# RG-LRU stage in another order of units, one subtraction per tile moved to GpSimd, and attention's first units begun block by block

## The chip, the cores and the metric

One NeuronCore of one Trainium2 chip. The metric is device time of one launch in microseconds (us), the median of three runs. Engines: TensorE (PE, its weight loads PEld), VectorE (DVE), ScalarE (ACT), GpSimd (POOL), SyncE (SP, which here only issues the DMAs of the weights).

## What is computed

Batch 1, 512 positions, width 1024, all in float32. Two blocks follow each other. The first has two layers (retention and gated delta net, then the RG-LRU), each followed by a convolved feed-forward; the second has two layers of attention (a stick-breaking half and a sliding-window half), each followed by an MLP. The part that matters here, cut from the reference:

```python
gate, xr = jnp.split(hn @ w_in, 2, axis=-1)
xr = causal_dwconv(xr, conv_w) + conv_b              # 4 taps
r = sigmoid(blockwise(xr, w_a) + b_a)                # 8 blocks of 128 x 128
i = sigmoid(blockwise(xr, w_x) + b_x)
log_a = -8.0 * r * softplus(-lam)
a = exp(log_a)
u = sqrt(-expm1(2.0 * log_a)) * (i * xr)
hs = linear recurrence hs[t] = a[t] * hs[t-1] + u[t]
y = (gelu(gate) * hs) @ w_out
...
h = rms_norm(x, g); proj = h @ w_in                  # attention: k, v, then q, k, v of each head pair
```

## The kernel before

Activations lie transposed, as 8 tiles of 128 channels by 512 positions. Every projection is a stream of **units**: one unit is a 128 x 1024 piece of weights that one DMA brings into `raw` (4 slots). ACT rounds it to `w_hi` (`w_split`, L848), DVE makes the rest `w_lo = raw - w_hi` (`w_low`, L1306), both with 3 slots, and PE multiplies it in 8 blocks. One block is three matmuls of 128x512 (`product`, L397 to L399: hi by hi, hi by lo, lo by hi), so a unit is 24 matmuls. The right-hand side is split the same way (`x_hi`, `x_lo`, `y_hi`, `y_lo`). `w_split` of unit u waits until unit u-3 is done on PE.

The order of each engine's work is written out by hand, and the engines wait for each other by counting semaphores; each engine works strictly in its own order. `wave` starts a stage whose input is still being made: it does blocks 0 to 6 of its first two units, each block waiting for its own input tile, then something in between, then block 7 of both.

**The recurrence stage** (about 780 to 900 us in the profile). PE multiplies eight `lru_x` units, two `lru_ax` units (each eight single blocks: for four tiles the weights of r and of i) and eight `lru_gate` units, then the `lru_out` wave. I call them x0 to x7, ax0 and ax1, g0 to g7, out0 to out7. For each x tile m:

- DVE scales the result into `lpad` and adds three taps (L1592); ACT makes the first tap (L1078) and `y_hi` (L1081); DVE makes `y_lo` (L1595). ax needs `y_hi`, `y_lo`.
- `lru_ri` (ACT, L1093, L1098): sigmoids of the ax results. `lru_decay` (ACT, L1108 to L1112): two Exp and a Tanh a tile, here called the three decay steps. `lru_root` (DVE), `lru_sqrt` (ACT), `lru_hs` and `lru_scan` (DVE, L1618, L1623), `lru_gelu` (ACT), then the last product and its hi and lo (DVE L1656, ACT L1147, DVE L1659), which block kk of out0 waits for as `lru_y` kk.

**The start of attention** (about 1292 and 2095 us). The last down units of the stage before make `x_hi`, `x_lo` and a running sum of squares tile by tile. PE waits for the last of that sum, multiplies it by ones (L680 and L681 at the first layer, L435 at the second), waits for tile 7 of x, and only then begins the units kv0, kv1 and the four units `pair` of head pair 0. Meanwhile ACT and DVE turn the sum into `scale`; at the first layer DVE then multiplies the 8 tiles of `h` by the norm (L1678) before it scales kv0. After kv1 is scaled PE transposes v (L788) and sums squares of k (L791). Then come four head pairs, each a fixed interleaving of stick-breaking, window and projection work (L739 is the first matmul of the window part).

Of the kernel before, what the change touches and what calls it, by code (L numbers as in the profile page):

```python
# [387 lines left out]
def pe_program(k):  # L388
# [278 lines left out]
    for half, between, after in ((0, ("lru_x", 5), [("lru_x", 6), ("lru_x", 7), ("lru_gate", 0)]),  # L667
                                 (1, ("lru_gate", 1), [("lru_gate", m) for m in range(2, LRU_TILES)])):
        lru_ax(half, 0)
        project(between, k.x_hi, k.x_lo, "pad" if half == 0 else "lru_g")  # L670
        lru_ax(half, 1)
        for name in after:
            project(name, k.x_hi, k.x_lo, "pad" if name[0] == "lru_x" else "lru_g")
# [5 lines left out]
    pe.wait_ge(*dve_done.at("ssum2", "final", KT - 1))  # L679
    pe.matmul(bank[7][:], k.ones, k.ssum[:], start=True, stop=True)  # L680
    pe.matmul(bank[6][:], k.ones, k.ssum2[:], start=True, stop=True).then_inc(*mark("norm", "final"))  # L681
    pe.wait_ge(*dve_done.at("x", "final", KT - 1))
# [1360 lines left out]
```

## Time and profile before

| | |
|---|---|
| median of three runs | 2897.78 us (2897.19 to 2903.42) |
| the profiled execution: its own time | 2902.6 us |
| its span in the trace | 2900.8 us |
| mean granted TensorE clock | 0.982 |
| PE busy | 2795.1 us, 96% of the span |
| DVE, ACT, POOL busy | 1512.1, 1167.5, 101.9 us |

The span runs from the first to the last instruction; the rest of the execution's own time lies around it. PE is busy 96% of the time, so what can be won is in its gaps and in the stretches at the lower clock.

### The profile page before, as it was taken

What the parts mean: (1) busy time and instruction counts of PE and PEld (TensorE: products, weight loads), DVE (VectorE), ACT (ScalarE), POOL (GpSimd) and SP (SyncE); (2) the same over time, 40 slices, a digit from 0 to 9 for tenths busy, and PEclk for the clock granted to TensorE, in tenths of its full rate; (3) what the DMA queues carried; (4) which work ended last, traced back from release to release, by engine and by line L of the source; (5) the groups of instructions that cost most, each with busy time, mean ns of one, the idle gap of its engine ahead of it and who ended that gap; (6) DMA issues with size and microseconds to landing.
All of it is one profiled execution on the core that took longest, in us unless ns stands there. A gap on an engine that the chain in (4) does not pass through costs nothing.

```text
span 2900.8 us, 30821 instructions
## 1 busy us (share of the span) xinstructions
PE 2795.1 (96%) x12462; PEld 2207.1 (76%) x12462; DVE 1512.1 (52%) x2085; ACT 1167.5 (40%) x1736; POOL 101.9 (4%) x71
## 2 busy tenths in 40 slices
PE   8999999999989999999999999999999999999999
PEld 6788868888867888876555788888765557888887
DVE  4666657565775746575334454443543344544433
ACT  6444344333474434353444433322434444333222
POOL 1333110000000000000000000000000000000000
PEclk9999999999999999999999999999999999999999
DMA  4111112323323322331111232223211112322232
GB/s 169 45 62 55 48 59 95 102 98 99 102 80 100 102 94 95 102 102 58 37 37 37 81 101 94 95 98 99 95 58 37 37 37 80 99 97 95 95 101 73
DMA packets 66812, 235.65 MB, mean 81 GB/s; under 512 B 7408, under 2 KB 8176, under 8 KB 66672
## 3 DMA queue, kind: packets, MB, share of 16 engines
q1 hardware_dynamic: 62064, 226.00, 23.8%
q10 hardware_dynamic: 4608, 7.70, 0.8%
q8 instruction: 99, 1.62, 0.2%
q14 instruction: 41, 0.34, 0.0%
HBM read 231.57 MB, written 2.10 MB: 81 GB/s over the span
## 4 chain that ended last, share of the span: by engine, by line
PE 88%; DVE 5%; ACT 4%; issue 1%; POOL 1%; ACTq 0%; DVEq 0%
PE bank L397 25%; PE bank L399 25%; PE bank L398 25%; PE bank L709 1%; PE bank L720 1%; PE bank L758 1%; ACT w_hi_k L848 1%; PE bank L700 1%; PE bank L712 1%; DVE w_lo_k L1306 1%; PE bank L769 1%; PE bank L530 1%; PE bank L776 1%; DVE xr_lru L1592 1%; POOL q_mix L1850 1%
## 5 line engine op out<-in xcount | busy, mean ns | idle before, releaser
L397 PE MATMUL bank<-x_hi_k,w_hi_k 128*128 128x512 f32 x2152 | 880.0, 409 | 17.6 <-DVE x_lo_k L1313 17.6
L848 ACT ACTIVATE w_hi_k<-raw_k 128x1024 fp32r<-128x1024 f32 x431 | 454.7, 1058 | 987.7 <-PE bank L399 987.7
L399 PE MATMUL bank<-x_hi_k,w_lo_k 128*128 128x512 f32 x2152 | 848.5, 394 | 0.0
L398 PE MATMUL bank<-x_lo_k,w_hi_k 128*128 128x512 f32 x2152 | 846.8, 393 | 0.0
L1306 DVE TENSOR_TENSOR w_lo_k<-raw_k,w_hi_k 128x1024 fp32r<-128x1024 f32 x431 | 530.4, 1231 | 177.2 <-ACT w_hi_k L848 176.9
L397 PEld LDWEIGHTS bank<-x_hi_k,w_hi_k 128*128 128x128 f32 x2152 | 410.6, 191 | 107.7 <-DVE x_lo_k L1313 21.0
L399 PEld LDWEIGHTS bank<-x_hi_k,w_lo_k 128*128 128x128 f32 x2152 | 408.6, 190 | 87.5
L398 PEld LDWEIGHTS bank<-x_lo_k,w_hi_k 128*128 128x128 f32 x2152 | 410.2, 191 | 85.4 <-issue 4.6
L397 PE MATMUL bank<-y_hi_k,w_hi_k 128*128 128x512 f32 x1136 | 447.8, 394 | 16.6 <-DVE w_lo_k L1306 7.6
L399 PE MATMUL bank<-y_hi_k,w_lo_k 128*128 128x512 f32 x1136 | 444.6, 391 | 0.0
L398 PE MATMUL bank<-y_lo_k,w_hi_k 128*128 128x512 f32 x1136 | 444.5, 391 | 0.0
L1334 DVE TENSOR_TENSOR h_k<-h_k,bank 128x512 f32<-128x512 f32 x136 | 93.4, 687 | 326.1 <-PE bank L399 325.8
L397 PEld LDWEIGHTS bank<-y_hi_k,w_hi_k 128*128 128x128 f32 x1136 | 214.5, 189 | 63.8 <-DVE w_lo_k L1306 8.0
L399 PEld LDWEIGHTS bank<-y_hi_k,w_lo_k 128*128 128x128 f32 x1136 | 214.5, 189 | 45.0
L398 PEld LDWEIGHTS bank<-y_lo_k,w_hi_k 128*128 128x128 f32 x1136 | 214.7, 189 | 43.8 <-issue 0.2
L1819 DVE SCALAR_TENSOR_TENSOR rel_att<-bank,scale_k 128x512 f32<-128x512 f32 x64 | 44.3, 692 | 158.5 <-PE bank L399 158.5
L1692 DVE SCALAR_TENSOR_TENSOR sp_t_att<-bank,e_t_att 128x128 f32<-128x128 f32 (+1 forms) x64 | 31.3, 489 | 95.4 <-ACT e_t_att L1192 94.6
L1197 ACT ACTIVATE w_t_att<-bank 128x128 f32<-128x128 f32 (+1 forms) x64 | 28.2, 440 | 116.4 <-PE bank L709 60.2
L1560 DVE SCALAR_TENSOR_TENSOR cv_ffn<-fpad_ffn,vec_k,cv_ffn 128x512 f32<-128x512 f32 x88 | 65.9, 749 | 1.5
L1560 DVE SCALAR_TENSOR_TENSOR cv_att<-fpad_att,vec_k,cv_att 128x512 f32<-128x512 f32 x88 | 65.9, 749 | 1.5
L700 PE MATMUL bank<-q_att,k_att 64*128 64x128 f32 (+3 forms) x128 | 55.1, 512 | 0.0
L1328 DVE TENSOR_TENSOR fpad_att<-bank,scale_k 128x512 f32<-128x512 f32 x44 | 30.3, 688 | 42.3 <-PE bank L399 42.3
(320 smaller groups left out, 2552.4 us busy)
## 6 DMA issues: line engine op xcount, KB each, us to landing
raw_k<-wstream SPq DMA_DIRECT2D x431, 512.0 KB, 3.3
h_k<-xT ACTq DMA_DIRECT2D x8, 256.0 KB, 8.1
outT<-h_k ACTq DMA_DIRECT2D x8, 256.0 KB, 2.8
decay_mix<-constants ACTq DMA_DIRECT2D x4, 256.0 KB, 2.6
levels_mix<-constants ACTq DMA_DIRECT2D x1, 448.0 KB, 9.1
vec_k<-vectors ACTq DMA_DIRECT2D x1, 286.5 KB, 4.4
cos_mix<-constants ACTq DMA_DIRECT2D x1, 256.0 KB, 8.7
sin_mix<-constants ACTq DMA_DIRECT2D x1, 256.0 KB, 8.6
```

Of the source, the lines that this page charges most:

```text
L397: pe.matmul(dst, wh, rh, start=start, stop=False)
L398: pe.matmul(dst, wh, rl, start=False, stop=False)
L399: return pe.matmul(dst, wl, rh, start=False, stop=stop)
L530: mm = pe.matmul(ch(bank[4], c), ch(k.um, c), ch(k.inv, c), start=True, stop=True)
L700: pe.matmul(z_view(k, j), k.ak[r, j * P:j * P + P], k.aq[r, j * P:T], start=True, stop=False)
L848: act.activation(k.w_hi[:, u % SPLIT, :], k.raw[:, u % RAW, :], ACT.Copy).then_inc(*hi_done.mark())
L1306: dve.tensor_tensor(k.w_lo[:, u % SPLIT, :], k.raw[:, u % RAW, :], k.w_hi[:, u % SPLIT, :].bitcast(F32), ALU.subtract).then_inc(*k.lo_done ...
L1328: return dve.tensor_tensor(dst, src, k.scale[:], ALU.mult).then_inc(*mark(*event))
L1334: dve.tensor_tensor(k.h[:, m, :], k.h[:, m, :], bank[BANK[name]][:], ALU.add).then_inc(*mark("added", u))
L1560: dve.scalar_tensor_tensor(cv[j][:], pad[j][:, s:s + T], vcol("ffn_conv", w0 + s), cv[j][:], ALU.mult, ALU.add).then_inc(*mark("conv", lay ...
L1692: dve.scalar_tensor_tensor(keys_view(k.sp_t, j), z_view(k, j), 0.0, k.e_t[:, n % 2, 0:T - j * P], ALU.max, ALU.add).then_inc(*mark("softpl ...
L1819: dve.scalar_tensor_tensor(k.rel[:, j, :], bank[i % 4][:], 0.0, k.scale[:], ALU.max, ALU.mult).then_inc(*mark("rel", u))
```

## The change

It has four parts.

1. **Recurrence, PE.** x5, x6 and g2 are each cut into blocks 0 to 3 and blocks 4 to 7. The order x4, ax0 (first half), x5, ax0 (second half), x6, x7, g0, ax1 (first half), g1, ax1 (second half), g2 becomes x4, x5 early, ax0 first half, x5 late, x6 early, ax0 second half, x6 late, x7, g0, ax1 first half, g1, g2 early, ax1 second half, g2 late.
2. **Recurrence, ACT and DVE.** Decay steps of tiles 0 and 1 stand inside x6 and x7, between tap and `y_hi`; those of 2 and 3 behind x7. `lru_sqrt(0)` moves behind the second round of sigmoids. `rr` has 8 tiles in place of 4, so the sigmoids no longer wait for `lru_hs`. DVE does multiplication and scan tile by tile, mixed with the gate units.
3. **Recurrence, GpSimd.** The subtraction that makes `y_lo` of the eight x tiles (L1595) leaves DVE and is done by POOL.
4. **Attention's start.** kv0 and kv1 become a `wave` with the sums in between. The units of head pair 0 get the banks 2, 3, 4 and 1. The multiplication of `h` at the first layer moves behind the scaling of kv0 and kv1, and ACT's root for k waits for it. The interleaving of the head pairs is as it was: stick over 0 to 1, window over 0 to 0.8, projections over 0.1 to 1.

```diff
+    for _n in range(4):
+        BANK["pair", _layer, 0, _n] = (2, 3, 4, 1)[_n]
...
-            pe.wait_ge(*dve_done.at("lru_xr", m))
+            pe.wait_ge(*k.pool_done.at("lru_xr", m))
...
+    def lru_part(name, event, ks):
+        blocks(UNIT[name], BANK[name], ks, k.x_hi, k.x_lo, KT)
+    early, late = range(4), range(4, KT)
+    lru_part(("lru_x", 5), "pad", early)
+    lru_ax(0, 0)
+    lru_part(("lru_x", 5), "pad", late)
+    lru_part(("lru_x", 6), "pad", early)
+    lru_ax(0, 1)
...
     def attention(layer):
-        first = Fill([("kv", layer, n) for n in range(2)] + [("pair", layer, 0, n) for n in range(4)], fill_piece)
-        first.part(8)
+        stage = ("att", 1) if layer == 1 else "final"
+        wave([("kv", layer, n) for n in range(2)], k.x_hi, k.x_lo, "fill", x_made(stage),
+             between=(lambda: sum_squares(bank[7][:], k.ssum, stage)) if layer == 1 else final_sums)
+        first = Fill([("pair", layer, 0, n) for n in range(4)], fill_piece)
+        first.part(4)
...
         act.wait_ge(*pe_done.at("wk_sum", layer))
+        if layer == 0:
+            act.wait_ge(*dve_done.at("h_final"))
...
-        dve.wait_ge(*act_done.at("lru_xr", m))
-        dve.tensor_tensor(k.y_lo[:, m, :], k.xr[:, m, :], k.y_hi[:, m, :].bitcast(F32),
-                          ALU.subtract).then_inc(*mark("lru_xr", m))
...
+        if layer == 0:
+            h_final(range(KT))
+        first.part(4)
...
+    for m in range(LRU_TILES):
+        pool.wait_ge(*k.act_done.at("lru_xr", m))
+        pool.tensor_tensor(k.y_lo[:, m, :], k.xr[:, m, :], k.y_hi[:, m, :].bitcast(F32),
+                           ALU.subtract).then_inc(*mark("lru_xr", m))
```

What ACT has in a row from the last sigmoids of the first round to the end of x7, before:

```order
L848 ACTIVATE w_hi_k<-raw_k 128x1024
L1108 ACT_TABLE_LOAD
L1108 ACTIVATE aa_lru<-rr_lru,c_lru 128x512
L1111 ACTIVATE aa_lru<-rr_lru,c_lru 128x512
L1112 ACTIVATE th_lru<-rr_lru,c_lru 128x512
L1108 ACTIVATE aa_lru<-rr_lru,c_lru 128x512
L1111 ACTIVATE aa_lru<-rr_lru,c_lru 128x512
L1112 ACTIVATE th_lru<-rr_lru,c_lru 128x512
L848 ACTIVATE w_hi_k<-raw_k 128x1024
L1078 ACTIVATE xr_lru<-pad_lru,vec_k 128x512
L1081 ACTIVATE y_hi_k<-xr_lru 128x512
```

And now (the lines have shifted: L862 is `w_split`, L1092 the tap, L1097 `y_hi`, L1121 to L1125 the decay steps):

```order
L862 ACTIVATE w_hi_k<-raw_k 128x1024 x2
L1092 ACTIVATE xr_lru<-pad_lru,vec_k 128x512
L1121 ACT_TABLE_LOAD
L1121 ACTIVATE aa_lru<-rr_lru,c_lru 128x512
L1124 ACTIVATE aa_lru<-rr_lru,c_lru 128x512
L1125 ACTIVATE th_lru<-rr_lru,c_lru 128x512
L1097 ACTIVATE y_hi_k<-xr_lru 128x512
L862 ACTIVATE w_hi_k<-raw_k 128x1024
L1092 ACTIVATE xr_lru<-pad_lru,vec_k 128x512
```

The weights of ax1 are the first single `w_hi` row of the new piece; three decay steps stand ahead of it where there were twelve (six here and six behind this `y_hi`).

What DVE has in a row at the end of the stage, before, from the scans of tiles 4 to 7 on:

```order
L1623 SCALAR_TENSOR_TENSOR xr_lru<-aa_lru,xr_lru 128x512 x4
L1328 TENSOR_TENSOR lru_g_k<-bank,scale_k 128x512
L1306 TENSOR_TENSOR w_lo_k<-raw_k,w_hi_k 128x1024
L1328 TENSOR_TENSOR lru_g_k<-bank,scale_k 128x512
L1306 TENSOR_TENSOR w_lo_k<-raw_k,w_hi_k 128x1024
L1656 TENSOR_TENSOR xr_lru<-xr_lru,lru_g_k 128x512 x2
L1659 TENSOR_TENSOR y_lo_k<-xr_lru,y_hi_k 128x512 x2
```

And now, from the first y on (L1638 and L1640 are multiplication and scan, L1352 the scaling of a gate, L1330 `w_low`, L1647 and L1650 the last product and its low part):

```order
L1647 TENSOR_TENSOR xr_lru<-xr_lru,lru_g_k 128x512 x2
L1650 TENSOR_TENSOR y_lo_k<-xr_lru,y_hi_k 128x512 x2
L1647 TENSOR_TENSOR xr_lru<-xr_lru,lru_g_k 128x512 x2
L1650 TENSOR_TENSOR y_lo_k<-xr_lru,y_hi_k 128x512 x2
L1638 TENSOR_TENSOR xr_lru<-xr_lru,rr_lru 128x512
L1640 SCALAR_TENSOR_TENSOR xr_lru<-aa_lru,xr_lru 128x512
L1638 TENSOR_TENSOR xr_lru<-xr_lru,rr_lru 128x512
L1640 SCALAR_TENSOR_TENSOR xr_lru<-aa_lru,xr_lru 128x512
L1352 TENSOR_TENSOR lru_g_k<-bank,scale_k 128x512
L1330 TENSOR_TENSOR w_lo_k<-raw_k,w_hi_k 128x1024
L1647 TENSOR_TENSOR xr_lru<-xr_lru,lru_g_k 128x512 x2
L1650 TENSOR_TENSOR y_lo_k<-xr_lru,y_hi_k 128x512 x2
```

Scans of tiles 6 and 7 and the scaling of g6 with its `w_lo` now stand between the y of tiles 2, 3 and the y of tiles 4, 5; before, all scans were done ahead of the first y.

PE at the first attention's start, with bank numbers, before (bank 3 is the last down unit, banks 7 and 6 take the sums, bank 0 is kv0):

```order
L398 MATMUL bank3<-y_lo_k_56,w_hi_k_50 128x512
L399 MATMUL bank3<-y_hi_k_55,w_lo_k_51 128x512
L680 MATMUL bank7<-ssum_k_57,con_k_59 128x512
L681 MATMUL bank6<-ssum2_att_135,con_k_59 128x512
L397 MATMUL bank0<-x_hi_k_53,w_hi_k_50 128x512
L398 MATMUL bank0<-x_lo_k_54,w_hi_k_50 128x512
```

And now (bank 1 is kv1, bank 2 the first pair unit):

```order
L401 MATMUL bank1<-x_hi_k_53,w_lo_k_51 128x512
L697 MATMUL bank7<-ssum_k_57,con_k_59 128x512
L698 MATMUL bank6<-ssum2_att_135,con_k_59 128x512
L399 MATMUL bank0<-x_hi_k_53,w_hi_k_50 128x512
L400 MATMUL bank0<-x_lo_k_54,w_hi_k_50 128x512
L401 MATMUL bank0<-x_hi_k_53,w_lo_k_51 128x512
L399 MATMUL bank1<-x_hi_k_53,w_hi_k_50 128x512
L400 MATMUL bank1<-x_lo_k_54,w_hi_k_50 128x512
L401 MATMUL bank1<-x_hi_k_53,w_lo_k_51 128x512
L399 MATMUL bank2<-x_hi_k_53,w_hi_k_50 128x512
```

The sums stand 14 blocks (42 matmuls) later than before.

## Rows read from the trace of the kernel before

**Rows 1.** The page, part 1: busy time of each engine.

```profile
PE 2795.1 (96%) x12462; PEld 2207.1 (76%) x12462; DVE 1512.1 (52%) x2085; ACT 1167.5 (40%) x1736; POOL 101.9 (4%) x71
```

**Rows 2.** Waits of PE: total us, times, longest.

```profile
PE bank L397 <- DVE w_lo_k L1306: 7.6, 1, 7.6
PE bank L680 <- DVE ssum_att L1322: 4.4, 1, 4.4
...
PE bank L435 <- DVE ssum_k L1319: 3.8, 1, 3.8
...
PE bank L397 <- DVE y_lo_k L1659: 3.1, 1, 3.1
PE bank L397 <- ACT xr_lru L1078: 2.8, 1, 2.8
PE bank L397 <- ACT rr_lru L1093: 1.9, 1, 1.9
PE bank L788 <- DVE wo_att L1771: 1.7, 2, 0.9
```

**Rows 3.** Windows of 10 us behind three PE waits: busy times, clock, DMA.

```profile
836.25:846.25 10.00, 10.00 (x33) 8.04 (x34) 7.31 (x11) 7.72 (x9) 0.00 (x0) 0.73 0.17 52
887.08:897.08 10.00, 10.00 (x32) 7.61 (x33) 5.55 (x9) 3.24 (x5) 0.00 (x0) 0.71 0.07 27
1296.62:1306.62 10.00, 10.00 (x28) 6.75 (x29) 3.69 (x7) 2.67 (x4) 0.00 (x0) 0.71 0.08 30
```

**Rows 4.** DVE timeline, recurrence: start, us, line, operation, [idle before].

```profile
797.77 1.22 DVE L1306 TENSOR_TENSOR w_lo_k<-raw_k,w_hi_k 128x1024 fp32r<-128x1024 f32 x1
...
834.98 1.22 DVE L1306 TENSOR_TENSOR w_lo_k<-raw_k,w_hi_k 128x1024 fp32r<-128x1024 f32 x1
...
864.76 2.50 DVE L1618 TENSOR_TENSOR xr_lru<-xr_lru,rr_lru 128x512 f32<-128x512 f32 x4 [0.89 <-ACT rr_lru L1119]
867.18 4.57 DVE L1623 TENSOR_TENSOR_SCAN xr_lru<-aa_lru,xr_lru 128x512 f32<-128x512 f32 x4
...
891.53 1.30 DVE L1659 TENSOR_TENSOR y_lo_k<-xr_lru,y_hi_k 128x512 fp32r<-128x512 f32 x2
```

**Rows 5.** ACT timeline, recurrence.

```profile
829.44 0.63 ACT L1081 ACTIVATE y_hi_k<-xr_lru 128x512 fp32r<-128x512 f32 x1 [2.55 <-DVE xr_lru L1592]
...
860.70 0.71 ACT L1112 ACTIVATE th_lru<-rr_lru,c_lru 128x512 f32<-128x512 f32 x1
861.32 1.04 ACT L848 ACTIVATE w_hi_k<-raw_k 128x1024 fp32r<-128x1024 f32 x1
862.38 1.28 ACT L1119 ACT_TABLE_LOAD   x1
863.67 2.01 ACT L1119 ACTIVATE rr_lru<-rr_lru 128x1024 f32<-128x1024 f32 x2
```

**Rows 6.** DVE and POOL timeline where both work, at about 400 us.

```profile
399.65 1.52 DVE L1306 TENSOR_TENSOR w_lo_k<-raw_k,w_hi_k 128x1024 fp32r<-128x1024 f32 x1
...
400.88 1.40 POOL L1872 TENSOR_TENSOR ssum_k<-ssum_k,sq_k 128x512 f32<-128x512 f32 x1 [0.80 <-ACT sq_k L874]
401.09 1.74 DVE L1313 SCALAR_TENSOR_TENSOR x_lo_k<-h_k,vec_k,x_hi_k 128x512 fp32r<-128x512 f32 x1
```

**Rows 7.** ACT and DVE timelines at the first attention's start.

```profile
1300.44 0.69 ACT L856 ACTIVATE rstd_k<-bank,eps_col_k 128x512 f32<-128x512 f32 x1 [3.95 <-PE bank L681]
...
1294.62 0.75 DVE L1313 SCALAR_TENSOR_TENSOR x_lo_k<-h_k,both_gains_att,x_hi_k 128x512 fp32r<-128x512 f32 x1
...
1305.42 5.39 DVE L1678 SCALAR_TENSOR_TENSOR h_k<-h_k,vec_k,rstd_k 128x512 f32<-128x512 f32 x8
```

**Rows 8.** Windows: head pairs 0, 1 and 2 of the first attention, columns as in rows 3.

```profile
1338.71:1409.22 70.51, 65.49 (x264) 42.31 (x264) 27.36 (x52) 30.98 (x68) 0.00 (x0) 0.93 0.12 38
1409.22:1481.14 71.92, 66.89 (x265) 42.70 (x265) 27.40 (x52) 30.98 (x68) 0.00 (x0) 0.91 0.11 37
1481.14:1547.68 66.54, 61.00 (x264) 39.33 (x264) 27.38 (x52) 30.75 (x68) 0.00 (x0) 1.00 0.12 40
```

More of the change, by code:

```diff
@@ L666, in pe_program, with final_sums @@
     pe.wait_ge(*act_done.at("scale", "lru"))
[L667 to L673, printed above, removed]
+    def lru_part(name, event, ks):
+        blocks(UNIT[name], BANK[name], ks, k.x_hi, k.x_lo, KT)
+        if ks[-1] == KT - 1:
+            emptied[BANK[name]] = (dve_done, (event, UNIT[name]))
+    early, late = range(4), range(4, KT)
[4 more added lines that the diff above has]
+    lru_ax(0, 1)
+    lru_part(("lru_x", 6), "pad", late)
+    project(("lru_x", 7), k.x_hi, k.x_lo, "pad")
+    project(("lru_gate", 0), k.x_hi, k.x_lo, "lru_g")
+    lru_ax(1, 0)
+    project(("lru_gate", 1), k.x_hi, k.x_lo, "lru_g")
+    lru_part(("lru_gate", 2), "lru_g", early)
+    lru_ax(1, 1)
+    lru_part(("lru_gate", 2), "lru_g", late)
+    for m in range(3, LRU_TILES):
+        project(("lru_gate", m), k.x_hi, k.x_lo, "lru_g")
     wave([("lru_out", m) for m in range(KT)], k.y_hi, k.y_lo, "added", lambda kk: ("lru_y", kk))
     conv_ffn(1)
[L679 to L682, printed above, removed]
+    def final_sums():
+        pe.wait_ge(*dve_done.at("ssum2", "final", KT - 1))
+        pe.matmul(bank[7][:], k.ones, k.ssum[:], start=True, stop=True)
+        pe.matmul(bank[6][:], k.ones, k.ssum2[:], start=True, stop=True).then_inc(*mark("norm", "final"))
     def stick(layer, pair):
@@ L1239, in attention @@
     def attention(layer):
-        first = Fill([("kv", layer, n) for n in range(2)] + [("pair", layer, 0, n) for n in range(4)], fill_piece)
-        first.part(8)
+        for n in range(2):
+            act.wait_ge(*unit_done.at(UNIT["kv", layer, n]))
+            w_split()
+        first = Fill([("pair", layer, 0, n) for n in range(4)], fill_piece)
         act.wait_ge(*dve_done.at("fill", UNIT["kv", layer, 1]))
@@ L1660, in dve_program @@
                               ALU.subtract).then_inc(*mark("lru_y", n))
+    for m in range(5):
+        lru_x(m)
+    lru_ix(0)
+    lru_x(5)
+    lru_ix(2)
+    w_low()
+    lru_x(6)
+    lru_root(0)
+    lru_x(7)
+    lru_root(1)
+    lru_root(2)
+    lru_root(3)
+    lru_gate(0)
+    lru_ix(4)
+    lru_gate(1)
+    lru_ix(6)
+    w_low()
+    lru_scan(0)
+    lru_scan(1)
+    lru_gate(2)
+    lru_scan(2)
+    lru_root(4)
+    lru_scan(3)
+    lru_root(5)
+    lru_gate(3)
+    lru_root(6)
+    lru_root(7)
+    lru_gate(4)
+    lru_scan(4)
+    lru_scan(5)
+    lru_gate(5)
+    lru_y(0)
+    lru_y(2)
+    lru_scan(6)
+    lru_scan(7)
+    lru_gate(6)
+    lru_y(4)
+    lru_gate(7)
+    lru_y(6)
     down([("lru_out", m) for m in range(KT)], ("ffn", 1), "norm_ffn", KT)
```

154 lines of the change are left out of this document (63 added, 91 removed).

## The prediction

> **What bounds the kernel now.** I read the page first, then PE's waits, then the clock behind the longest of them, then the DVE and ACT timelines around them. PE is busy for 2795.1 of 2900.8 us [rows 1], and the change removes no matmul, so it can only win PE's idle time and the time lost at the lower clock. The list of waits shows where the idle time is that the change touches [rows 2]. In the recurrence: 2.8 (ax0, first half), 1.9 (ax0, second half), 7.6 (ax1), 3.1 (out0), together 15.4 us. At the two starts of attention: 4.4 and 3.8 us for the last sum of squares, and 1.7 us in two for v. Behind the waits of 7.6, 3.1 and 4.4 PE runs 10 us at a granted clock of 0.73, 0.71 and 0.71 [rows 3]: a mix of the levels 2.4 and 1.2 GHz. I take the same 0.71 behind the wait of 3.8. At a mean of 0.71, 10 us hold 7.1 us of full-speed work, so each such wait costs 2.7 to 2.9 us more. One matmul starts every 0.227 us at full clock (the page's mean, with the small ones, is 2795.1 / 12462 = 0.224 [rows 1]), so a block is 0.68 and a unit 5.44 us.
>
> The names of the releasers need care: the 2.8 us are put down to `xr_lru`, but the weights' low part of ax0 ended at 797.77 + 1.22 = 798.99 [rows 4], when PE went on. And ax1 began at 836.25 when its `w_lo` ended, 834.98 + 1.22 = 836.20 [rows 3, 4].
>
> **Attention, second layer: 7.5 us.** The wave fills the wait for the last sum with 14 blocks (9.5 us) whose x tiles are ready. So the 3.8 us go, with them the 2.9 us of clock, and the 0.8 us for v as well, since scaling of kv0 and kv1 now lies beside the first pair unit. 3.8 + 2.9 + 0.8 = 7.5.
>
> **Attention, first layer: 7.4 us.** PE is free at 1296.62 - 4.35 = 1292.27. Tile 7 of x is made at 1294.62 + 0.75 = 1295.37 [rows 7]; it is wanted behind 14 blocks, at 1301.8. The sums take 1.8 us (two matmuls in float32, four passes each), then two blocks to 1305.0, the first pair unit to 1310.4. The chain from the sums to `scale` took from 1300.44 to 1305.42, where the product on `h` began [rows 7]: 5.0 us. From 1303.7 it ends at 1308.7. kv0's scaling, `w_lo`, kv1's scaling are 0.6 + 1.1 + 0.7, so kv1 is there at 1311.2 and PE waits 0.8 us in place of 0.9. Gain: 4.4 + 2.9 + 0.1 = 7.4. The moved product on `h` (5.4 us, eight instructions of 0.67 [rows 7]) ends at about 1317.6. Behind it on DVE queue the first pair unit's scaling and a `w_lo`; behind it on ACT the root for k (1.3 us), since that overwrites `rstd`. Then k's rotation (six dependent steps of 0.72 and a scaling) and v's scaling: to 1328.3, while PE ends the fourth pair unit at 1328.8. So the cover is 0.5 us; what runs over it is paid one for one by the first head pair.
>
> **Recurrence, up to ax1.** I laid the new order out with the durations of the rows, noting each engine's next free time.
> - ax0 first half comes behind half of x5, at 796.2 + 2.7 = 798.9, when its weights are there (798.3 to 799.2): wait at most 0.3 in place of 2.8.
> - ax0 second half waits for the first sigmoid, which ACT starts only behind x4 and a table load (1.28 [rows 5]): done at 809.3 as before. PE comes at 807.4: wait 2.1, but half of x6 is already behind it.
> - g0 waits 0.5 for weights.
> - ax1's weights: twelve decay steps of 0.62 (860.70 to 861.32 [rows 5]) stood ahead of them on ACT. Now three do, and they lie in the 2.55 us in which ACT waited for the taps [rows 5]. 12 x 0.62 = 7.4, so the weights end at 828.8, not 836.2. PE comes at 826.6: wait 2.2 in place of 7.6, and too short to bring the clock down (2.8 did not).
> - g2 waits 0.8: its weights now stand behind six decay steps.
>
> **Recurrence, the end.** ax1's second half starts at 840.7, its last sigmoid ends at 844.4. From there ACT has, to the weights of out0, five `w_hi` (1.0 each), four table loads (1.35 with the drain ahead), four square roots (0.95), twelve decay steps (0.62), two gelus (1.0), 0.2 of waiting: 23.8 us [rows 5], so `w_lo` of out0 ends at 869.3. From there DVE is full: y of tiles 0 to 3, eight instructions of 0.60 (2.4 for four, 864.76 to 867.18) and 0.4 of waiting, 5.2; two products and scans (0.60 + 1.14 + 0.12), 3.7 [rows 4]; g6 and a `w_lo`, 1.7; then y of 4 is ready at 882.0, y of 5 at 882.6; g7 and a `w_lo` and y of 6 by 886.4. PE leaves g7 at 873.3 (840.7 + 5.4 + 27.2), does four blocks of out0 to 876.1 and waits 5.9 for y 4 and, after two blocks, about 2 to 3 for y 6. That is a new wait, 8 us where 3.1 was. The first part will bring the clock down. From y 6 on, nine blocks (6.1 us): before from 892.3 (y 6, from 891.53 [rows 4]), now from 886.4. With about 0.9 us of clock in either case the gain is 5.9, less 0.2 for rounding of the layout: **5.7 us**. The ledger agrees: idle 15.4 and clock 5.6 before, idle 13.6 and clock about 1.7 after.
>
> **GpSimd.** The eight subtractions leave DVE (0.60 each), but the x tiles' rhythm was set by `y_hi`, `w_hi`, `w_lo`, taps, which stay; 5.36 a tile becomes 5.1 if nothing collides. A POOL instruction of this size takes 1.40, and DVE ones beside it stretched: a `w_lo` took 1.52 where 1.22 is usual, an `x_lo` 1.74 where 0.75 is usual [rows 4, 6, 7]. The new subtraction overlaps the next `w_lo` by 0.4, as in the first case, so I take 0.3 each: 5.4 a tile, as before. Six such overlaps lie on the path. Bounds: nothing each, gain 7.4; 1.0 each, gain about 2. The Trainium skill (SBUF — State Buffer, "SBUF: two separate sides") has it that a DVE instruction with two SBUF inputs and a GpSimd one that reads SBUF exclude each other for a whole instruction; by that each `w_lo` would start 0.45 later and the gain would be 4.9. Perfetto Trace Analysis in the same skill ("Optimizing Scalar/DVE Operations") warns that moving work between these two might not help; the rows of 400 us agree that it is not free.
>
> **Sum.** 7.5 + 7.4 + 5.7 = 20.6 us off the profiled execution's 2902.6: 2882.0. That one stands 4.8 us above the median of the runs shown, 2897.78; from the median it is 2877.2. I say **2877**.
>
> **The rivals.**
> - *As laid out* (0.64), own range 2870 to 2884.
> - *The port costs whole instructions and the new wait holds the clock down longer* (0.12): gain 2 less 1.6 in the recurrence. The `x_lo` of 1.74 speaks for it; the overlap, which falls on another spot, against it. 20.6 - 5.3 = 15.3: 2882 to 2883.
> - *The head pairs' clock.* Pairs 0, 1, 2 have the same work and take 70.5, 71.9 and 66.5 us at clocks of 0.93, 0.91, 1.00 [rows 8]. The change moves their start by about 13 us at the first layer and does not touch their waits, so this share is drawn anew, by a mechanism outside the change. Kinder (0.10): the two slow ones lose their 4.0 and 5.4, the second layer's two likewise: up to 15 more, 2862 to 2869. Harsher (0.07): each of eight as slow as pair 1: some 13 less, 2890.
> - *It does not do it at attention* (0.04): DVE, with the product on `h` before pair 0's land, overruns its 0.5 us of cover, or kv1's scaling comes late at both layers. 5 us less, 2882; against it, every x tile but the last is ready when PE is free.
> - *Slower* (0.03): the clock of the head pairs again, but held down throughout. Pair 1 was low for 18% of 71.9 us, 12.9 us, and lost 5.4: 0.42 a us. It decides where eight pairs lose 26.4 us more than now (20.6 and the 5.8 of the bound below), 3.3 a pair more than the mean of 3.1 that the three rows show, which is above the worst row. At 8 us a pair it would be 39 more: 2916. Against it: no pair shows it.
>
> **How the numbers follow.** 0.2% is 5.8 us, about what a measurement here can tell from no change. The range 2866 to 2886 takes in the bounds of the port (minus 3.7, plus 1.7), of the clock in the recurrence (minus 1.6, plus 0.9), and most of the pairs' clock; outside lie the harsher pairs, the slower case, and the kindest end: about 0.2. Faster needs under 2892.0: all but the last case and a corner of the harsher one.
>
> **What the profile after would show.** Right: no wait of PE over 1 us between 1270 and 1320 shifted by about 6, and the clock at 1.00 there; ax1 waiting about 2; a wait of about 6 in out0, put down to the low part of y, and one of 2 to 3 behind it; `w_lo` in the x tiles 1.2 to 1.6. Wrong: a wait at the x6 or g0 weights over 1 us (the port costs more), `w_lo` of out0 later than 871, or the first pair's start waiting for v's scaling. It would be wrong in size if the pairs sum to more than 10 us off their present time.

## The result, and the profile after

The changed kernel takes 2879.58 us (median of 14 runs, 2873.92 to 2893.69); the kernel before took 2897.49 beside it (14 runs, 2894.98 to 2906.71). The ratio is 0.9944, with a 95% interval of 0.9929 to 0.9958: 17.9 us faster, where 20.6 was forecast. The profiled execution took 2876.39 (span 2874.8, mean granted clock 0.988), against 2902.6 before (span 2900.8, clock 0.982).

The page, part 1, of the changed kernel, then PE's waits (total us, times, longest):

```profile
PE 2781.6 (97%) x12462; PEld 2198.0 (76%) x12462; DVE 1508.6 (52%) x2077; ACT 1166.4 (41%) x1736; POOL 112.3 (4%) x79
```

```profile
PE bank L399 <- DVE x_lo_k L1337: 17.1, 6, 12.2
PE bank L769 <- DVE wq_att L1751: 14.5, 8, 1.8
PE bank L785 <- DVE p_t_att L1781: 14.4, 13, 1.5
PE bank L755 <- ACT sq_k L1230: 13.8, 8, 1.7
PE bank L399 <- DVE y_lo_k L1650: 7.1, 2, 5.7
...
PE bank L399 <- DVE w_lo_k L1330: 2.3, 2, 1.9
PE bank L399 <- ACT rr_lru L1107: 1.9, 1, 1.9
...
PE bank L807 <- DVE wo_att L1804: 0.6, 1, 0.6
```

Against [rows 2], both waits for a last sum of squares (4.4, 3.8) are gone, as is the 2.8, and the 7.6 for ax1 has become 1.9. The wait for the low part of y has grown from 3.1 to 7.1 us, in two waits. The same waits in PE's timeline (start, us, line, [idle before <- releaser]):

```profile
826.79 0.50 PE L399 MATMUL bank<-y_hi_k,w_hi_k 128*128 128x512 f32 x1 [1.93 <-DVE w_lo_k L1330]
880.61 0.80 PE L399 MATMUL bank<-y_hi_k,w_hi_k 128*128 128x512 f32 x1 [5.66 <-DVE y_lo_k L1650]
885.01 0.80 PE L399 MATMUL bank<-y_hi_k,w_hi_k 128*128 128x512 f32 x1 [1.48 <-DVE y_lo_k L1650]
1305.44 0.66 PE L807 MATMUL bank<-con_k,wo_att 128*128 128x128 f32 x4 [0.65 <-DVE wo_att L1804]
1325.32 1.12 PE L755 MATMUL bank<-sq_k,con_k 128*128 128x512 f32 x2 [1.73 <-ACT sq_k L1230]
```

I call a time at a granted clock of 0.50, the level of 1.2 GHz, a low stretch. Windows of PE (columns as in [rows 3]): the low stretch behind ax1, ten us behind the wait in out0, and where attention starts:

```profile
827.87:831.28 3.41, 3.41 (x10) 2.64 (x9) 1.67 (x3) 2.28 (x4) 1.29 (x1) 0.50 0.41 144
...
880.61:890.61 10.00, 8.52 (x22) 6.28 (x23) 4.86 (x7) 3.06 (x4) 0.00 (x0) 0.57 0.25 84
...
1295.00:1305.00 10.00, 9.80 (x40) 7.08 (x38) 4.11 (x6) 4.58 (x6) 0.00 (x0) 1.00 0.00 0
```

At attention the clock stays at 1.00, where it was 0.71 before. Behind out0's wait the mean is 0.57, lower than any of [rows 3]: the clock is at 0.50 until 889.3. GpSimd's new work, and the DVE instruction beside it:

```profile
784.97 1.48 DVE L1330 TENSOR_TENSOR w_lo_k<-raw_k,w_hi_k 128x1024 fp32r<-128x1024 f32 x1 [1.05 <-ACT w_hi_k L862]
...
784.07 1.30 POOL L1910 TENSOR_TENSOR y_lo_k<-xr_lru,y_hi_k 128x512 fp32r<-128x512 f32 x1 [371.73 <-ACT y_hi_k L1097]
789.43 1.30 POOL L1910 TENSOR_TENSOR y_lo_k<-xr_lru,y_hi_k 128x512 fp32r<-128x512 f32 x1 [4.06 <-ACT y_hi_k L1097]
```

**Where the 26.0 us between the two spans are.** I cut both traces at the first scaling into `pad_lru` (781.09 before, 779.27 after), at the first addition of an out unit to h (899.04, 893.48), and at the first matmul of each layer's first head pair (1338.71 and 2140.06; 1325.32 and 2114.64).

```profile
893.48 0.69 DVE L1358 TENSOR_TENSOR h_k<-h_k,bank 128x512 f32<-128x512 f32 x1 [7.92 <-PE bank L401]
```

Ahead of the recurrence, where nothing was edited, 1.8. The recurrence 117.95 to 114.21: 3.7. From there to the first pair 439.67 to 431.84: 7.8. From pair to pair 801.35 to 789.32: 12.0, in which the second layer's start and the first layer's pairs lie together. The first three pairs take 205.19 where they took 208.97, which is 3.8 of it. The last 360 matmuls ahead of the second layer's first pair take 92.22 (clock 0.96) before and 83.89 (clock 1.00) after, which is 8.3:

```profile
2047.84:2140.06 92.22, 85.67 (x362) 68.61 (x360) 44.39 (x56) 32.13 (x43) 0.00 (x0) 0.96 0.26 86
...
2030.75:2114.64 83.89, 82.17 (x361) 67.04 (x360) 44.38 (x56) 32.03 (x43) 0.00 (x0) 1.00 0.30 94
```

The rest is 0.6 behind the second layer's first pair. So the three places of the change show 3.7 + 7.8 + 8.3 = 19.8, and some 6 of the 26 are work that the change does not touch.

The runs themselves say this too. Those of the changed kernel at a mean clock of 0.989 or 0.990 take 2873.9 to 2876.4, those at 0.981 take 2893.1 to 2893.7, one program. The scatter of 20 us goes with the clock.

### The profile page after: what moved, and what is told of

Same layout as the page of the kernel before. It is cut to its first block, busy times and chain, and to the rows that moved or that the text cites. A ratio compares the mean times of both kernels' runs of the same rounds, so it can differ in the third digit from the quotient of the medians.

```text
span 2874.8 us, 30831 instructions
## 1 busy us (share of the span) xinstructions
PE 2781.6 (97%) x12462; PEld 2198.0 (76%) x12462; DVE 1508.6 (52%) x2077; ACT 1166.4 (41%) x1736; POOL 112.3 (4%) x79
## 4 chain that ended last, share of the span: by engine, by line
PE 87%; DVE 5%; ACT 5%; issue 2%; POOL 1%; ACTq 0%; DVEq 0%
PE bank L399 25%; PE bank L401 25%; PE bank L400 25%; PE bank L725 1%; ACT w_hi_k L862 1%; PE bank L736 1%; PE bank L774 1%; DVE w_lo_k L1330 1%; PE bank L716 1%; PE bank L728 1%; PE bank L785 1%; PE bank L532 1%; PE bank L792 1%; POOL q_mix L1885 1%; POOL v_mix L1885 1%
## 5 line engine op out<-in xcount | busy, mean ns | idle before, releaser
L862 ACT ACTIVATE w_hi_k<-raw_k 128x1024 fp32r<-128x1024 f32 x431 | 454.2, 1058 | 949.0 <-PE bank L401 949.0
L1330 DVE TENSOR_TENSOR w_lo_k<-raw_k,w_hi_k 128x1024 fp32r<-128x1024 f32 x431 | 531.7, 1234 | 182.0 <-ACT w_hi_k L862 181.6
L1352 DVE TENSOR_TENSOR fpad_att<-bank,scale_k 128x512 f32<-128x512 f32 x44 | 30.3, 688 | 42.3 <-PE bank L401 42.3
```

The source lines that it names most:

```text
L862: act.activation(k.w_hi[:, u % SPLIT, :], k.raw[:, u % RAW, :], ACT.Copy).then_inc(*hi_done.mark())
L1330: dve.tensor_tensor(k.w_lo[:, u % SPLIT, :], k.raw[:, u % RAW, :], k.w_hi[:, u % SPLIT, :].bitcast(F32), ALU.subtract).then_inc(*k.lo_done ...
L1352: return dve.tensor_tensor(dst, src, k.scale[:], ALU.mult).then_inc(*mark(*event))
```

## The experiments

Each was measured beside the kernel before, in sets on different chips. Where a time is compared with the changed kernel's 2879.6 and not with the kernel before, the few us by which the sets differ stand in it. "Stage" is the recurrence between the first two cuts, of the one profiled execution.

| kernel | median us (lowest to highest, runs) | ratio to before, 95% | stage us |
|---|---|---|---|
| before | 2897.5 to 2900.9 by set | 1 | 117.95 |
| changed | 2879.6 (2873.9 to 2893.7, 14) | 0.9944 [0.9929, 0.9958] | 114.21 |
| lru_only | 2895.1 (2887.9 to 2900.8, 12) | 0.9979 [0.9967, 0.9990] | 111.52 |
| att_only | 2880.2 (2878.5 to 2886.5, 6) | 0.9942 [0.9928, 0.9955] | 118.08 |
| no_pool | 2880.6 (2876.5 to 2883.5, 6) | 0.9939 [0.9925, 0.9953] | 114.39 |
| old_decay | 2886.6 (2884.7 to 2887.2, 5) | 0.9957 [0.9945, 0.9969] | 121.79 |
| dec_only | 2882.8 (2880.8 to 2890.8, 6) | 0.9944 [0.9926, 0.9962] | 119.44 |
| yo_pool | 2887.7 (2882.5 to 2896.4, 12) | 0.9965 [0.9951, 0.9978] | 116.87 |
| h_first | 2886.0 (2884.5 to 2890.4, 5) | 0.9955 [0.9938, 0.9972] | 111.49 |
| pairs_90 | 2880.4 (2880.2 to 2882.5, 5) | 0.9933 [0.9915, 0.9951] | 111.48 |
| pairs_05_95 | 2928.0 (2926.2 to 2928.8, 4) | 1.0095 [1.0076, 1.0113] | 111.49 |
| pairs_gap1 | 2846.4 (2843.5 to 2846.7, 4) | 0.9811 [0.9792, 0.9829] | 111.48 |
| pairs_gap2 | 2873.5 (2871.9 to 2874.4, 6) | 0.9905 [0.9888, 0.9921] | 113.06 |
| before_gap1 | 2864.0 (2863.2 to 2867.2, 4) | 0.9884 [0.9866, 0.9901] | 117.09 |

### The two parts alone: lru_only and att_only

`lru_only` has the diff's hunks for the recurrence alone, `att_only` those for attention's start alone (the wave for kv0 and kv1, the sums behind 14 blocks, the product on h moved).

> Only the recurrence's parts of the change; attention starts as before. Theory (gains add up, each at its own place): 4 to 6 us less than before, and in the trace the waits of the changed kernel in the recurrence (about 1.9, 1.9, 5.7, 1.5 us) with the old waits of 4.4 and 3.8 us at attention's starts. Rival (the new wait of 5.7 us at out0 and the low clock behind it take back what the others give, all gain is attention's): 0 to 2 us less. Rival (the recurrence gives most of it): 10 us or more less.

> Only attention's parts of the change; the recurrence as before. Theory: 15 to 16 us less than before (7.5 at each layer), give or take some 5 us for the clock in the head pairs. Rival (gain is the recurrence's): under 8 us less. If attention and recurrence share a cause (the clock in the head pairs being drawn anew by any shift), the two runs' gains would not add to the change's 18.

In `lru_only` the stage falls by 6.4 us and both waits for sums stay (4.35 and 3.75). Whole times: 5.8 below the kernel before on the same chip, as the theory had it. In `att_only` the recurrence is as before (118.08, ax1 waits 7.52), and from the stage's end to the first pair it takes 1331.74 - 899.90 = 431.84, which is the changed kernel's to the hundredth. So attention's first start is worth 7.8 by itself. By stages the two gains stand apart. By whole times they do not add: `att_only` is 20.7 below the kernel before on that chip and `lru_only` 5.8, together 26.5, where the change shows 17.9. That is the third case of the expectation. The medians of `att_only` and of the changed kernel can't be told from each other, so that whole times alone do not show that the recurrence's part adds anything to attention's: its 4 to 6 us are within what the clock of the head pairs moves, and only the stage shows them.

### The recurrence: no_pool, old_decay, dec_only

`no_pool` puts the low parts of the x tiles back on DVE:

```
 def lru_x(m):                       # dve_program
...
+        dve.wait_ge(*act_done.at("lru_xr", m))
+        dve.tensor_tensor(k.y_lo[:, m, :], k.xr[:, m, :], k.y_hi[:, m, :].bitcast(F32),
+                          ALU.subtract).then_inc(*mark("lru_xr", m))
...
-    for m in range(LRU_TILES):      # pool_program
-        pool.wait_ge(*k.act_done.at("lru_xr", m))
-        pool.tensor_tensor(k.y_lo[:, m, :], ...
```

> The changed kernel with the low parts of the x tiles back on DVE. Theory (the move to GpSimd gives back what it saves, since the w_lo beside it stretches from 1.22 to 1.48): the tiles' rhythm stays at 5.36 us, wait at ax1 2.8 in place of 1.9, y of tile 7 in out0 0.3 to 1 us later; in time the same as the changed kernel within 1.5 us. Rival (eight instructions of 0.60 us less on a full DVE are 4.8 us): 4 to 5 us slower than the changed kernel. Rival (the port costs more than the move saves): faster by 1 to 2 us.

Little changes: from the stage's start to the end of PE's second wait for y it is 105.68 us here, 105.74 in the changed kernel. But a low stretch fell behind ax0 here and behind ax1 there. The five other profiles of the changed recurrence with the stretch behind ax0 (`lru_only`, `h_first`, `pairs_90`, `pairs_05_95`, `pairs_gap1`) have 105.0. Like against like, the move is worth 0.6 to 0.7 us, within the 0.3 to 1 that was expected; the stretched `w_lo` gives most of the 4.8 us back.

`old_decay` keeps the new orders, but puts ACT's decay steps of tiles 0 to 3 (and their roots on DVE) where they were:

```
+    lru_decay(0)
+    lru_decay(1)
+    lru_x(6)
-    lru_x(6, 0)
-    lru_x(7, 1)
     lru_decay(2)
     lru_decay(3)
+    lru_x(7)
```

> The changed kernel with the decay steps of tiles 0 to 3 where they stood before: 0 and 1 ahead of x6, 2 and 3 ahead of x7. Theory (the twelve steps on ACT set when ax1's weights are there, and the delay runs through to the end of the stage): wait at ax1 about 10 us in place of 1.9, low part of y of tile 7 some 7 us later, whole kernel 5 to 7 us slower than the changed one. Rival (the cut of PE's units is what gives the time, ACT's order is hidden): within 2 us of the changed kernel.

ax1 waits 8.68, everything behind it is late, and the stage takes 121.79: 7.6 more than the changed kernel's and 3.8 more than before. PE's units are cut in halves here as in the changed kernel, so the halves do not give the gain by themselves. From this I took the decay steps to be the whole gain. `dec_only` was to show it: on `att_only`, with the kernel before's orders, only the decay steps go behind the x tiles:

```
     lru_ri(0, 1)
-    lru_decay(0)
     lru_x(6)
-    lru_decay(2)
+    lru_decay(0)
     lru_x(7)
+    lru_decay(2)
     lru_sqrt(0)
```

> The attention part of the change, and of the recurrence's only this: ACT's first twelve decay steps go behind the x tiles 6 and 7 rather than ahead of and between them, and DVE's two pairs of roots with them. Orders of the units on PE, scans, y, gelus, GpSimd as before. Theory A (what the recurrence gains comes from the decay steps that stood ahead of ax1's weights; the rest of its edits add little): ax1's wait falls from 7.6 to 1 to 3 us, the wait in out0 grows from 3.1 to 6 or more since DVE's scans now end the stage, the stage lasts 114 to 115.5 us (before 118.0, changed 114.2), the time is 2879 to 2883. Rival B (only with the new orders at the end does the earlier ax1 carry through): the stage lasts 116.5 or more, the time 2883 to 2887. Rival C (the halves of x5, x6 and the new end are a loss of their own): the stage under 113.5, the time 2878 or less.

Theory A fell; the stage is rival B's (116.5 or more). PE's timeline of `dec_only`, then ACT's behind the last decay steps:

```profile
833.24 0.50 PE L399 MATMUL bank<-y_hi_k,w_hi_k 128*128 128x512 f32 x1 [2.78 <-DVE w_lo_k L1309]
846.18 0.76 PE L399 MATMUL bank<-y_hi_k,w_hi_k 128*128 128x512 f32 x1 [4.48 <-ACT rr_lru L1093]
```

```profile
839.79 1.28 ACT L1119 ACT_TABLE_LOAD   x1
841.08 2.00 ACT L1119 ACTIVATE rr_lru<-rr_lru 128x1024 f32<-128x1024 f32 x2
842.99 1.04 ACT L848 ACTIVATE w_hi_k<-raw_k 128x1024 fp32r<-128x1024 f32 x1
844.05 1.28 ACT L1093 ACT_TABLE_LOAD   x1
845.35 0.69 ACT L1093 ACTIVATE rr_lru<-bank,vec_k 128x512 f32<-128x512 f32 x1
```

ax1 waits 4.8 us less, and its second half waits 4.5 for the sigmoid, which on ACT now stands behind the rest of the decay steps, the square roots and two table loads. PE's idle time in the stage is 2.8 + 1.9 + 2.8 + 4.5 + 3.1 + 0.3 = 15.4, as much as before, and the stage is 1.5 longer. In the changed kernel that queue is shorter by the square roots and one table load, which stand behind the second round of sigmoids, and the steps of tiles 0 and 1 lie inside x6 and x7, in the times in which ACT waits for the taps; those of tiles 2 and 3 still stand ahead of ax1's sigmoids. Which of these edits counts for how much, and whether PE's halves are needed beside them, no run separates. Neither half of the reordering is worth anything alone: 119.4 with the steps alone, 121.8 with the orders alone, 111.5 to 114.4 with both.

### The end of the recurrence: yo_pool

The eight low parts of y go to GpSimd too:

```
-        for n in range(m, m + 2):   # dve_program, lru_y
-            dve.wait_ge(*act_done.at("lru_y", n))
-            dve.tensor_tensor(k.y_lo[:, n, :], ...
+    for m in range(LRU_TILES):      # pool_program
+        pool.wait_ge(*k.act_done.at("lru_y", m))
+        pool.tensor_tensor(k.y_lo[:, m, :], ...
```

> The changed kernel, with the eight low parts of the out inputs (y_lo of tiles 0 to 7, at the recurrence's end) on GpSimd too instead of DVE; the x tiles as changed. Theory A (DVE is the full engine between w_lo of out0 and the y of tile 7, so the wait of 5.7 us in out0 is made of DVE's queue): DVE sheds 8 x 0.60, of which 4 to 6 lie ahead of the y on which PE waits; a GpSimd instruction of 1.3 lies behind each y_hi instead of 0.6, which takes 0.7 back at each point of use. The wait of 5.7 falls to 3 to 4, the stage gets 2 to 2.5 us shorter (114.2 to about 112), the time 1 to 3 us below the changed kernel's 2879.6. Rival B (the chain is gelu, product, y_hi, y_lo, and GpSimd's longer instruction sits in it; or DVE's instructions beside GpSimd's stretch from 0.60 to 0.8): the wait stays at 5 to 7 and the stage at 114 or longer, the time 0 to 2 us above.

Rival B's kind, but dearer than it said: 8 us above the changed kernel's median where it had 0 to 2. PE waits for y four times (0.71, 1.17, 4.61 and 2.00, sum 8.5) in place of twice (7.1), the clock is low from 876.5 to 893.5, and the stage lasts 5.4 longer than the 111.49 that five kernels with the same recurrence show. DVE's and GpSimd's timelines of `yo_pool`:

```profile
871.21 1.78 DVE L1639 TENSOR_TENSOR xr_lru<-xr_lru,rr_lru 128x512 f32<-128x512 f32 x1
873.02 2.18 DVE L1641 TENSOR_TENSOR_SCAN xr_lru<-aa_lru,xr_lru 128x512 f32<-128x512 f32 x1
875.13 1.68 DVE L1639 TENSOR_TENSOR xr_lru<-xr_lru,rr_lru 128x512 f32<-128x512 f32 x1
876.84 1.22 DVE L1641 TENSOR_TENSOR_SCAN xr_lru<-aa_lru,xr_lru 128x512 f32<-128x512 f32 x1
...
869.11 7.15 POOL L1911 TENSOR_TENSOR y_lo_k<-xr_lru,y_hi_k 128x512 fp32r<-128x512 f32 x4 [37.54 <-ACT y_hi_k L1146]
```

Four subtractions take 7.15 (1.79 each, 1.30 at the x tiles), and a DVE multiplication beside them 1.78 where the changed kernel shows 0.68, a scan 2.18 where 1.22 is usual. The second scan, behind the last of the four, is at 1.22 again. Each of the first three DVE instructions lost about 1 us, not much under a whole GpSimd instruction. The Trainium skill (SBUF — State Buffer, "SBUF: two separate sides") has it that of a DVE instruction with two SBUF inputs and a GpSimd one that reads SBUF, whichever starts first keeps the pair of ports that they share for the whole instruction, and the other waits. The trace agrees here; at the x tiles the two overlap by only 0.40 us and DVE has idle time, and 0.26 a tile was all it cost.

### Attention's cover: h_first

```
+    h_final(range(KT))              # ahead of attention's scaling of kv0, kv1
...
-        if layer == 0:
-            h_final(range(KT))
```

> The changed kernel, with the eight products on h at the first attention (5.39 us together on DVE) ahead of kv0's and kv1's scaling rather than behind them. Theory A (the order on DVE behind the scale decides the wait for v, as the prediction had it): kv1's scaling comes 5.4 us later, PE has about 5 us of the first pair's units that do not need it only where its program puts them, so the wait for v of 0.65 becomes 5.5 to 6.5, the clock falls behind it for 2 to 3 us more of loss, layer 0's start is 7 to 9 us later, and the time is 5 to 9 us above the changed kernel's. Rival B (the wait for v has slack behind, or PE is fed by the pair units meanwhile): the wait grows by under 2, the time stays within 2 us. Neither expects a change at layer 1.

Theory A. The product on h takes 5.39 us from 1301.45, kv1's scaling starts at 1308.49, and PE waits 5.95 for it instead of 0.65:

```profile
1309.23 1.11 PE L807 MATMUL bank<-con_k,wo_att 128*128 128x128 f32 x4 [5.95 <-DVE wo_att L1806]
```

Stage's end to the first pair is 1331.20 - 891.97 = 439.2, 7.4 more, of which 5.3 is the wait; the other 2.1 are the clock's, 0.74 over the 10 us from 1309. Without moving this product the change would have gained next to nothing at the first layer.

### The head pairs: pairs_90, pairs_05_95, pairs_gap1, pairs_gap2, before_gap1

Since their clock makes the scatter, I tested what brings it down. In the changed kernel each pair has a wait of 1.73 at its start and one of 1.82 for wq 9 us later, and its low stretches begin just behind (the first pair: at 1336.5, 2.1 us behind the end of the wait for wq; clock 0.67 over 1340 to 1350). First two that only stretch shares in `pair_tasks`; the changed kernel has 0 to 0.8 for the window and 0.1 to 1 for the filling:

```
-    return ((stick, STICK_STEPS, 0, 1), (window, WINDOW_STEPS, 0, 0.8),
+    return ((stick, STICK_STEPS, 0, 1), (window, WINDOW_STEPS, 0, 0.9),       # pairs_90
+    return ((stick, STICK_STEPS, 0, 1), (window, WINDOW_STEPS, 0.05, 0.95),   # pairs_05_95,
+            (filling(...), len(fill.units) * PARTS, 0, 1))                     # filling too
```

> The changed kernel, with the sliding window part of each head pair spread over 0 to 0.9 of the pair's order of steps rather than 0 to 0.8. Theory A (a pair's time is its matmuls at the clock that is granted, and the clock falls at the waits of 1.5 to 1.8 us that recur in each pair: p_t of the window, wq, sq_k at the start): with the window's waits further apart there is filling between them, total waits of PE on p_t_att (14.4 us) fall by 5 or more, the mean clock comes up to about 0.990 in every run, and the time is 5 to 10 us below, with a smaller spread. Rival B (waits move to another place: the last steps of the window run against the end of the filling): waits on p_t_att stay at 12 to 18, pairs' mean stays at 68 to 70 us, time within 4 us. Rival C: the window's end now comes in the way of the next pair's start (sq_k wait grows from 1.7), 5 to 10 us slower.

> The changed kernel, with the window over 0.05 to 0.95 of each head pair's order of steps and the filling over 0 to 1 (before 0 to 0.8 and 0.1 to 1). Theory A (filling ahead of the first waits of a pair covers the wait for sq_k and wq): the sq_k wait of 1.7 at each of eight pair starts falls below 1, 5 us of PE idle go, clock 0.99 or above, 5 to 12 us faster. Rival B: the filling's units use up cover at the pair's start which is missing at its end, waits of 1.5 turn up there; within 4 us. Rival C: the filling needs weights whose low parts are made on DVE just then, and waits for them by 2 to 5 us a pair: 10 us slower or more.

`pairs_90` takes PE's waits for `p_t` from 14.4 to 4.5 us, but the one for wq grows (17.2 in eight, 2.2 the longest), all eight pairs go low behind it, and the time is the changed kernel's with hardly any scatter (2.3 us). Rival B in its time, though not in its waits. `pairs_05_95` is 48 us worse: the start wait is gone, wq's is 2.7, `p_t`'s 2.7, and two new ones of 1.3 and 1.4 (`k_att`, `w_t_att`) come in every pair. Rival C's sign, not its cause.

Then an empty step more between the window's first product and the scores that wait for wq, so that one filling part of two blocks falls there (`pairs_gap1`; two steps and 0.95 in `pairs_gap2`), on all three engines alike:

```
-WINDOW_STEPS = 2 + 2 + 2 * 6 + 1
+WINDOW_STEPS = 2 + 2 + 1 + 2 * 6 + 1
...
-(window, WINDOW_STEPS, 0, 0.8)
+(window, WINDOW_STEPS, 0, 0.9)
...
         k.sq, start=True, stop=True).then_inc(*mark("wq_sum", *at))
+        yield
```

> The changed kernel with the window over 0 to 0.9 of each head pair's order, and one empty step more between a pair's first window product (the sum for wq) and the scores that wait for wq. Theory A (the wq wait of 2.15 us that the stretch to 0.9 left, 9 us behind the pair's start wait of 1.77, is what brings the clock down in each pair; low stretches begin right behind it): one filling part of two blocks, 1.4 us, now lies in it, the wait falls to 0.9 or less, the low stretches of the pairs (74 us in all there, 61 in the changed kernel) fall below 40, the mean clock reaches 0.990 and the time is 2862 to 2870. Rival B (the clock falls from the pair's small products and its many waits together): the wait falls, low stretches stay at 60 or more, the time falls by at most the idle, 8 x 1.3 = 10 us at best, less what comes back at the pair's end: 2873 to 2880. Rival C (a late window pushes its end onto the next pair's start): over 2882.

> As with one empty step, but two, and the window over 0 to 0.95. Theory A: the wq wait is gone, and only the pair's start wait of 1.7 is left: low stretches below 25 us in all pairs, the time 2855 to 2866. Rival B: low stretches of 60 or more though the waits are gone, 2870 to 2878. Rival C: the window's last products and the output of the pair stand against the next pair's start, and its wait grows from 1.8 to 3 or more: over 2882.

`pairs_gap1` takes 2846.36, 33 us below the changed kernel, 54 below the one before, and 34 below `pairs_90`, from which it differs only by the step. Its waits:

```profile
PE bank L755 <- ACT sq_k L1231: 14.2, 8, 1.8
PE bank L786 <- DVE p_t_att L1784: 8.6, 16, 0.6
...
PE bank L716 <- ACT w_t_att L1219: 3.9, 8, 0.5
```

The wait for wq (14.5 us in eight) is off the list, and none within a pair is over 0.6. Of that the idle time explains 16 us (14.5 and 5.8 of `p_t` gone, 3.9 of `w_t` new and 0.4 more at the start). The rest is the clock: the eight pairs have 10.2 us of low stretches where the changed kernel's have 41.0, and 30.8 us at half speed are 15.4. (The expectation's 61 and 74 us for the changed kernel and `pairs_90` are 41.0 and 68.3 in the traces.) Windows of its pairs 0, 1 and 2 in the first layer:

```profile
1325.36:1389.71 64.35, 61.01 (x265) 39.45 (x265) 26.95 (x52) 30.58 (x68) 0.00 (x0) 1.00 0.13 41
1389.71:1455.63 65.92, 62.58 (x265) 40.59 (x265) 27.23 (x52) 30.59 (x68) 0.00 (x0) 0.97 0.12 40
1455.63:1519.97 64.34, 61.00 (x264) 39.45 (x264) 26.95 (x52) 30.59 (x68) 0.00 (x0) 1.00 0.13 42
```

194.6 us for three pairs, which were 205.2; full clock in two. The start wait of 1.77 is still there; behind it the clock goes low in three of the eight pairs, for 3.4 us each (at 1390.9, 2100.8 and 2295.4), where with both waits it went low in six of the eight, for 3.4 to 10.2. Its time is below theory A's range: the clock's part is as large as A's whole gain (10 to 18 us), and the 16 us of idle time come on top. `pairs_gap2` shows the other side:

```profile
PE bank L787 <- DVE p_t_att L1787: 32.5, 16, 2.8
```

The wait has moved on to `p_t`, 2.8 at its longest, with a low stretch of 3.4 us at it in each of the eight pairs, and 27 us are back. That is rival C's kind, but within the pair: the next pair's start waits 1.8 as ever. Its time, 2873.5, lies in rival B's range, but B had the waits gone.

Last, the pairs' order of `pairs_gap1` on the kernel before, so that the change can be priced with quiet pairs.

> The kernel before, with the head pairs' order of pairs_gap1 and nothing of the change: its pairs keep full clock nearly throughout, so that against pairs_gap1 (2846.4) it shows what the change itself is worth without the pairs' clock. Theory A (the pairs' clock is outside the change, whose parts add: recurrence 3.7 as the profiles had it, layer 0's start 7.8, layer 1's 7.5): 19 to 20 us above pairs_gap1, 2865 to 2867. By the prediction's sum, 5.7 for the recurrence: 2867. Rival B (part of what the change showed came through a lucky draw of the pairs' clock): 12 to 16 above, 2858 to 2862. Rival C (the head pairs were worse after the change's shift, and hid some of its gain): 24 or more, over 2870. PE's waits before pair 0 as in the kernel before.

2863.98 against 2846.36, 17.6 apart, between the two theories' ranges, and the cuts say where. Stage 117.09 and 111.48: 5.6. To the first pair 439.96 and 432.32: 7.6. Pair to pair 781.25 and 773.94: 7.3. Together 20.5; ahead of the stage and behind the second layer's first pair `pairs_gap1` is 0.8 and 1.6 slower, in places that are the same in both programs. Behind it `pairs_gap1` has two low stretches in its pairs and `before_gap1` one.

## Why the prediction was right, and where its steps were off

**The bound and the sign: right.** No matmul was removed (x12462 in both), PE is at 97%, and the gain is idle time and clock at the three places that were named.

**Attention, second layer, 7.5: right.** 8.3 in the first pair of profiles, 7.3 with quiet pairs. The kernel before had 6.8 us of low stretch at its wait for the sum in the first case and 3.4 in the second. The waits for the sum and for v are off the list.

**Attention, first layer, 7.4: right.** 7.8 in the first pair of profiles, 7.6 in the quiet one. PE waits 0.65 for v where 0.8 was worked out, the clock keeps 1.00. That the product on h had to leave DVE's queue, and that 0.5 us of cover would do behind it, is shown by `h_first` and by the start wait of pair 0, 1.73 as in the other pairs.

**Recurrence, 5.7: the layout right, the clock mis-sized, the sum in part luck.** The layout held: ax1 at 1.93 (2.2 said), the wait in out0 5.66 (5.9), then 1.48 (2 to 3), y 6 at 105.7 from the stage's start (105.3). The wait of 0.8 at g2 was not there in the profiled execution and 0.6 in the others. The failing term is "about 0.9 us of clock in either case", in the ledger "clock about 1.7 after". Low stretches at out0 and PE behind its second wait, first in the changed kernel, then in `pairs_gap1`:

```profile
879.07:889.31 10.24, 7.22 (x16) 5.25 (x17) 6.30 (x10) 4.47 (x6) 0.00 (x0) 0.50 0.35 104
885.01:889.31 4.30, 4.29 (x10) 3.43 (x11) 0.55 (x1) 0.00 (x0) 0.00 (x0) 0.50 0.14 54
```

```profile
878.85:885.68 6.83, 2.93 (x6) 1.82 (x6) 6.74 (x10) 3.75 (x5) 0.00 (x0) 0.50 0.27 86
886.57:893.04 6.47, 6.47 (x28) 5.37 (x29) 0.55 (x1) 0.00 (x0) 0.00 (x0) 1.00 0.07 27
```

Both begin while PE still waits for y 4 (to 880.61 and 882.16). In the changed kernel PE worked 3.4 us (ax1) and 7.2 us (out0) at half speed, which loses 5.3 us; in `pairs_gap1` it was 3.4 and 2.9, which loses 3.2. Against that the waits of the stage sum to 11.3 and 10.6 us where the ledger had 13.6. The two errors offset each other: 3.7 us gained in the profiled execution, 5.6 to 6.6 in the five others at 111.5, and `pairs_gap2`, with the same recurrence, lies between at 113.06. That 5.7 lies among these is in part luck, and so is how close the quiet pair's 5.6 comes.

Of the 2.7 us between 114.21 and 111.5, 0.7 lie ahead of the end of the second wait for y (105.7 against 105.0 from the stage's start) and 2.0 behind it. In the changed kernel 4.3 us of the low stretch lie behind that end, in `no_pool` 4.8 and in `pairs_gap2` 3.5, and from there to the stage's end it takes 8.47, 8.71 and 8.08; where the stretch is over by then, in the five, it takes 6.47. One wait, two prices, by how much of the low stretch lies behind the last wait of the stage.

**"Too short to bring the clock down (2.8 did not)": wrong.** Behind ax1's wait of 1.93 the clock went low at 827.87 (the window of 0.50 above); in the five others it had gone low behind the 1.87 at ax0, and ax1 waited about 1.05. And in `before_gap1`, behind the very wait of 2.8 on which the sentence rested:

```profile
799.12:802.53 3.41, 3.41 (x10) 2.67 (x9) 2.64 (x5) 1.58 (x2) 0.00 (x0) 0.50 0.48 154
```

One profile's silence on a short wait was one draw. PE loses 1.7 us in such a stretch, but the next wait can take it up: in `before_gap1` ax0's second half then waited 0.30 in place of 1.86, and the five with the stretch behind ax0 reach the end of the second wait for y at 105.0, as does `pairs_gap2`, which has no such stretch. Behind ax1, in the changed kernel, it came out as 0.7 us.

**ax1's twelve decay steps: right as a sum, incomplete as a cause.** The prediction told the gain as 12 x 0.62 that leave the path. `dec_only` shows that this by itself only hands the wait to the next sigmoid.

**GpSimd, 0.3 an x tile: right** (1.48 where 1.22 was: 0.26), and the rhythm is 5.36 where 5.4 was forecast. By the Trainium skill's rule as the prediction read it each `w_lo` would have come 0.45 later; at the x tiles the trace was kinder than that by 0.19, and at y (`yo_pool`) it shows nearly the whole instruction.

**The head pairs' clock as a rival outside the change: right in kind.** It made the median's gain 17.9 where the three places show 20.5 in the quiet pair, and 26.2 in the first profiles. That it could be steered by one filling part was not seen; with it named as the largest unknown, its waits should have been looked at too. The prices of this rival are mis-summed: the two slow pairs' 4.0 and 5.4 at two layers are 18.8, not 15, and eight pairs at 5.4 in place of the mean 3.1 are 18 more, not 13, which from 2877 is 2895 and above the 2892.0 up to which the prediction called it faster. The forecast does not hang on them, but three of the 14 runs of the changed kernel (2893.1 to 2893.7) lie there, outside its range.

## What to carry to other kernels

Taking work from ahead of a late instruction pays only if the next instruction that the same engine owes is not behind it: follow the engine's queue to the second customer before adding up the gain. Here two short waits of 1.7 to 1.8 us, 9 us apart, cost more than their sum, since the clock fell behind the second; closing it with one filling part was worth more than the whole reordering (34 us against 18). And where one profile stands for a program whose clock is drawn anew in each run, price a change by its stages, cut at the same instructions in both traces, and compare those.
